# First mixer of a two-block model: gate and convolved projections as one stream of 28 three-pass tiles, with scan and norms inside it

## What is computed

```python
h = rms_norm(x, norm_in_gain) * (1.0 + scale) + shift
q, k, v, z_attn, xbc, dt_raw, z_ssm = jnp.split(h @ w_in, splits, axis=-1)
o = stick_breaking_attention(q, k, v)
y_attn = rms_norm(o, sb_norm_gain) * jax.nn.silu(z_attn)
xbc = jax.nn.silu(causal_depthwise_conv(xbc, conv_w, conv_b))     # 4 taps, 1536 channels
xs, b_ssm, c_ssm = jnp.split(xbc, ...)                            # 1024, 256, 256
dt = jax.nn.softplus(dt_raw + dt_bias); a = -jnp.exp(a_log)
y = ssd_scan(xs, dt, a, b_ssm, c_ssm, d_skip)                     # Mamba-2, chunked, 16 heads of 64
y_ssm = rms_norm(y * jax.nn.silu(z_ssm), ssm_norm_gain)
x = x + gate * (jnp.concatenate([y_attn, y_ssm], -1) @ w_out)
```

## Time and profile before

| | |
|---|---|
| median of 3 runs | 2508.65 us (2505.75 to 2510.89) |
| profiled execution | 2508.63 us, of which the span is 2506.8 us |
| mean granted TensorE clock | 0.928 of full speed |
| busy over the span | PE 2208.9 us, DVE 1297.9, ACT 751.9, POOL 164.7 |
| attention's end to first w_out matmul | 346.28 to 669.50 us of the span |

### The profile page before, as it was taken

The page is one execution under the profiler, slowest core; times in us unless marked ns, Lnnn a source line. Parts: engine busy times, 40 slices in busy tenths (PEclk is TensorE's granted clock), DMA queues, the critical chain, the costliest instruction groups (busy, mean ns, idle before and its releaser), DMA issues. The chain is left out here.

```text
span 2506.8 us, 36778 instructions
## 1 busy us (share of the span) xinstructions
PE 2208.9 (88%) x15962; PEld 1677.8 (67%) x15962; DVE 1297.9 (52%) x1857; ACT 751.9 (30%) x1098; POOL 164.7 (7%) x137
## 2 busy tenths in 40 slices
PE   6998998968796994999899799989894997999896
PEld 2885754766585861899826688878452665888784
DVE  2325733675335457545533667633377635676434
ACT  2334631222322442010012322222243633222222
POOL 0000000000000007211130000000003400000000
PEclk8998999978898996999979899999987998999998
DMA  6222001201131220000002132323320011323230
GB/s 251 101 93 76 1 19 66 77 9 34 52 100 61 101 70 0 4 4 4 16 17 68 59 100 94 101 79 98 101 70 1 1 59 42 99 95 100 78 100 34
DMA packets 45841, 158.79 MB, mean 63 GB/s; under 512 B 5120, under 2 KB 7168, under 8 KB 45552
## 3 DMA queue, kind: packets, MB, share of 16 engines
q1 hardware_dynamic: 43824, 150.84, 18.4%
q10 hardware_dynamic: 1856, 5.60, 0.6%
HBM read 154.28 MB, written 2.14 MB: 62 GB/s over the span
## 5 line engine op out<-in xcount | busy, mean ns | idle before, releaser
L883 PE MATMUL banks<-up_x_high,up_w_high 128*128 128x512 f32 x704 | 276.3, 392 | 29.1 <-DVE up_x_low L896 29.1
L884 PE MATMUL banks<-up_x_low,up_w_high 128*128 128x512 f32 x704 | 275.9, 392 | 0.0
L885 PE MATMUL banks<-up_x_high,up_w_low 128*128 128x512 f32 x704 | 275.6, 392 | 0.0
L866 DVE TENSOR_TENSOR up_w_low<-weight_ring,up_w_high 128x1024 fp32r<-128x1024 f32 x88 | 107.8, 1226 | 140.1 <-ACT up_w_high L861 140.1
L883 PEld LDWEIGHTS banks<-up_x_high,up_w_high 128*128 128x128 f32 x704 | 133.4, 190 | 58.5 <-issue 30.7
L904 DVE SCALAR_TENSOR_TENSOR act<-banks,cols,act 128x511 f32<-128x511 f32 (+2 forms) x212 | 158.8, 749 | 7.5
L885 PEld LDWEIGHTS banks<-up_x_high,up_w_low 128*128 128x128 f32 x704 | 133.4, 190 | 28.2
L884 PEld LDWEIGHTS banks<-up_x_low,up_w_high 128*128 128x128 f32 x704 | 133.5, 190 | 27.5
L318 PE MATMUL banks<-down_x_high,down_w_high 128*128 128x512 f32 x352 | 139.5, 396 | 13.1 <-DVE down_x_low L357 13.1
L861 ACT CAST up_w_high<-weight_ring 128x1024 fp32r<-128x1024 f32 x88 | 92.1, 1049 | 192.8 <-PE banks L885 188.4
L319 PE MATMUL banks<-down_x_low,down_w_high 128*128 128x512 f32 x352 | 139.1, 395 | 0.0
(11 more groups left out here) (445 smaller groups left out, 4814.0 us busy)
## 6 DMA issues: line engine op xcount, KB each, us to landing
weight_ring<-in_up SPq DMA_DIRECT2D x88, 512.0 KB, 3.6
weight_ring<-in_down SPq DMA_DIRECT2D x44, 512.0 KB, 3.6
weight_ring<-in_w_ada SPq DMA_DIRECT2D x24, 512.0 KB, 5.9
weight_ring<-in_w_rkv SPq DMA_DIRECT2D x24, 512.0 KB, 3.2
weight_ring<-in_w_in SPq DMA_DIRECT2D x20, 512.0 KB, 3.3
weight_ring<-in_w_out SPq DMA_DIRECT2D x16, 512.0 KB, 3.2
weight_ring<-in_w_q SPq DMA_DIRECT2D x8, 512.0 KB, 6.8
weight_ring<-in_w_k SPq DMA_DIRECT2D x8, 512.0 KB, 3.2
```

The source lines that it names most:

```text
L866: nc.vector.tensor_tensor(w_low[:, n % 2, :], ring[:, i % RING, :], w_high[:, n % 2, :].bitcast(f32), ALU.subtract).then_inc(wl_made, 1)
L883: nc.tensor.matmul(PS[:, n % 4, :], high, x_high[:, k, :], start=k == 0, stop=False)
L884: nc.tensor.matmul(PS[:, n % 4, :], high, x_low[:, k, :], start=False, stop=False)
L885: mm = nc.tensor.matmul(PS[:, n % 4, :], low, x_high[:, k, :], start=False, stop=k == 7)
```

## The change

Stages 1 to 7, up to w_out, become one block with one queue per engine, written out by hand. After dt, TensorE runs a stream of 28 three-pass tiles: 12 of xbc, 8 of z_ssm, 8 of z_attn (now three-pass too; z_ssm becomes tile-wise, with w_z laid out in tiles like the others). x_high and x_low of all eight tiles of h are made once and kept. The tiles z0 to z15 use banks 6 and 7. The scan's matmuls stand between gate tiles: per chunk the inputs with broadcasts 0 and 1, a gate tile, broadcasts 2 and 3, two gate tiles, the outputs and the state (pairs of heads interleaved). Broadcasts use two banks (4 and 5) in place of four. The sums of the attention norm follow tile 3, those of the scan's norm follow z13. VectorE makes w_low of tiles 0 and 1 alone; GpSimd makes the other 26 and multiplies y_attn by its gates. ScalarE makes a tile's w_high right after taking the tile two before it (take_z). norm_ssm is finished before the w_out block begins. Removed lines of the scan that return as they were are left out here, as is the rest that "..." stands for; take_z, high_of_weights and chunk are functions of ScalarE's queue.

```diff
         planned(A["w_ada"], range(16, 24), 8)
-        planned(A["w_in"], range(20), 8)
         planned(A["w_dt"], range(1), 8, 16)
+        planned(A["w_in"], range(8, 20), 8)
         planned(A["w_z"], range(8), 8)
+        planned(A["w_in"], range(8), 8)
         planned(A["w_out"], range(16), 8)
...
-        run_stage(norm_program("norm_sb", rows(o), 8, D, 1e-6, lambda i: col("sb_norm_gain", i), rows(y_attn), scratch=rows(F[4]))[0],
-                  gemm_program("z_attn", 8, 8, rows(h), {"act": lambda e, n, b: nc.scalar.activation(F[3][:, n, :], b, ACT.Silu)}))
-        multiply("gate_attn", y_attn[:, :, :], y_attn[:, :, :], F[3][:, :, :])
-        xs, bc = F[3], F[4]
-        run_stage(conv_program("xbc", 12, None, 4, lambda n, j: col("conv_w", j * 12 + n), lambda n: col("conv_b", n),
-                               lambda n: xs[:, n, :] if n < 8 else bc[:, n - 8, :], split=(*open_split("xbc", 5, KT), rows(h), None)))
...
+        y_attn, xs, bc = F[2], F[3], F[4]
+        x_high, x_low, w_high, w_low = open_split("hproj", 5, KT)
...
+        AFTER = [(1, 2, 3), (4, 5, 6), (7, 8, 9), (10, 11, 12)]
...
+        def gate(pool, j):
+            pool.wait_ge(z_taken, j + 1)
+            pool.wait_ge(o_scaled, j - 7)
+            nc.gpsimd.tensor_tensor(y_attn[:, j - 8, :], y_attn[:, j - 8, :], z_dst(j), ALU.mult).then_inc(z_gated, 1)
...
+                def passes(t, k, bank):
+                    high, low = (w[:, t % 2, k * P:(k + 1) * P] for w in (w_high, w_low))
+                    nc.tensor.matmul(PS[:, bank, :], high, x_high[:, k, :], start=k == 0, stop=False)
+                    nc.tensor.matmul(PS[:, bank, :], high, x_low[:, k, :], start=False, stop=False)
+                    return nc.tensor.matmul(PS[:, bank, :], low, x_high[:, k, :], start=False, stop=k == 7)
+
+                def z_tile(j):
+                    next_chunk(pe)
+                    pe.wait_ge(wl_made, N_XBC + j + 1)
+                    if j >= 2:
+                        pe.wait_ge(z_taken, j - 1)
+                    for k in range(8):
+                        mm = passes(N_XBC + j, k, 6 + j % 2)
+                    mm.then_inc(weight_used, 1)
...
+                def broadcasts(c, quarters):
+                    for q4 in quarters:
+                        if q4 >= 2:
+                            pe.wait_ge(sca[c], 4 + 2 * (q4 - 2))
+                            pe.wait_ge(vec[c], 7 + 2 * (q4 - 2))
...
+                    if c:
+                        pe.wait_ge(vec[c - 1], 29)
...
+                    if c:
+                        pe.wait_ge(vec[c - 1], 32)
+                    broadcasts(c, (0, 1))
...
+                def chunk_outputs(c):
+                    for pair in range(H // 2):
+                        if pair % 2 == 0:
+                            pe.wait_ge(vec[c], 15 + pair)
...
+                next_chunk(pe)
+                next_chunk(pe)
+                pe.wait_ge(wl_made, 2)
+                for k in range(8):
+                    pe.wait_ge(xl_made, k + 1)
+                    for t in range(2):
+                        mm = passes(t, k, t)
+                        if k == 7:
+                            mm.then_inc(weight_used, 1)
+                for t in range(2, N_XBC):
+                    next_chunk(pe)
+                    pe.wait_ge(wl_made, t + 1)
+                    if t >= 4:
+                        pe.wait_ge(conv_step, TAPS * (t - 3))
+                    for k in range(8):
+                        mm = passes(t, k, t % 4)
+                    mm.then_inc(weight_used, 1)
+                    if t == 3:
...
+                z_tile(0)
+                for c in range(NB):
+                    chunk_inputs(c)
+                    z_tile(AFTER[c][0])
+                    broadcasts(c, (2, 3))
+                    z_tile(AFTER[c][1])
+                    z_tile(AFTER[c][2])
+                    chunk_outputs(c)
+                z_tile(13)
...
+                z_tile(14)
+                z_tile(15)
...
+                def high_of_weights(t):
+                    i = first + 1 + t
+                    act.wait_ge(weight_loaded[i % RING], 16 * (i // RING + 1))
+                    if t >= 2:
+                        tile_done(act, t - 2)
+                    nc.scalar.copy(w_high[:, t % 2, :], ring[:, i % RING, :]).then_inc(wh_made, 1)
+
+                def take_z(j):
+                    tile_done(act, N_XBC + j)
+                    if j >= 11:
+                        act.wait_ge(z_gated, j - 10)
+                    nc.scalar.activation(z_dst(j), PS[:, 6 + j % 2, :], ACT.Silu).then_inc(z_taken, 1)
+                    if j + 2 < 16:
+                        high_of_weights(N_XBC + j + 2)
...
+                high_of_weights(0)
+                high_of_weights(1)
+                for k in range(8):
+                    nc.scalar.copy(x_high[:, k, :], h[:, k, :]).then_inc(xh_made, 1)
...
+                for i in range(8):
+                    nc.scalar.activation(sq_o(i), y_attn[:, i, :], ACT.Square, scale=D ** -0.5).then_inc(o_squared, 1)
+                for t in range(N_XBC):
+                    high_of_weights(t + 2)
...
+                    act.wait_ge(conv_step, TAPS * (t + 1))
+                    nc.scalar.activation(conv_dst(t), conv_dst(t), ACT.Silu).then_inc(conv_silu, 1)
+                take_z(0)
+                for c in range(NB):
+                    chunk(c)
+                    for j in AFTER[c]:
+                        take_z(j)
+                take_z(13)
+                for i in range(8):
+                    act.wait_ge(s_gated, i + 1)
+                    nc.scalar.activation(sq_o(i), y[:, i, :], ACT.Square, scale=D ** -0.5).then_inc(s_squared, 1)
+                act.wait_ge(s_summed, 1)
+                nc.scalar.activation(root, sum_bank, ACT.Abs_reciprocal_sqrt, bias=eps_col).then_inc(s_rooted, 1)
+                take_z(14)
+                take_z(15)
...
+                for n in range(N_XBC):
+                    convolve(n)
...
+                    if n >= 6 and n < 10:
+                        for i in (2 * (n - 6), 2 * (n - 6) + 1):
+                            nc.vector.scalar_tensor_tensor(out=y_attn[:, i, :], in0=y_attn[:, i, :], scalar=col("sb_norm_gain", i), in1=root,
+                                                           op0=ALU.mult, op1=ALU.mult).then_inc(o_scaled, 1)
...
+                for c in range(NB):
+                    chunk(c)
+                dve.wait_ge(z_taken, 8)
+                dve.wait_ge(vec[NB - 1], 29)
+                for i in range(8):
+                    nc.vector.tensor_tensor(y[:, i, :], y[:, i, :], z_ssm[i], ALU.mult).then_inc(s_gated, 1)
...
+            @block.gpsimd
+            def _(pool):
+                for t in range(2, N_TILES):
+                    pool.wait_ge(wh_made, t + 1)
+                    nc.gpsimd.tensor_tensor(w_low[:, t % 2, :], ring[:, (first + 1 + t) % RING, :], w_high[:, t % 2, :].bitcast(f32), ALU.subtract).then_inc(wl_made, 1)
+                    j = t - N_XBC - 2
+                    if j >= 8:
+                        gate(pool, j)
+                gate(pool, 14)
+                gate(pool, 15)
...
-        split_gemm("z_ssm", 8, rows(h), {"act": lambda e, n, b: nc.scalar.activation(F[3][:, n, :], b, ACT.Silu)})
-        multiply("gate_ssm", F[3][:, :, :], F[3][:, :, :], y[:, :, :])
...
-        run_stage(norm_ssm, split_chain("w_out",
+        run_stage(split_chain("w_out",
```

More of the change, by code:

```diff
@@ new lines, in program @@
+        sdt = flat(h)
+        state, x_dt, x_end = sdt[:, 0:1024], sdt[:, 1024:2048], sdt[:, 2048:3072]
+        b_tok, cb = sdt[:, 3072:3328], sdt[:, 3328:3584]
+        seg, c_exp = wide[:, 0:2048], wide[:, 2048:4096]
+        y = xs
+        z_ssm = [bc[:, 4 + i, :] for i in range(4)] + [aux[:, i * T:(i + 1) * T] for i in range(4)]
+        z_attn = [aux[:, (4 + i) * T:(5 + i) * T] for i in range(3)]
+        z_dst = lambda j: z_ssm[j] if j < 8 else z_attn[j % 3]
+        slot = lambda i: late[:, 512 + i * 64:576 + i * 64]
@@ new lines, in program @@
+        s_gated, s_squared, s_summed, s_rooted, s_fixed, s_scaled = (sem("norm_ssm_" + n) for n in ("gated", "squared", "summed", "rooted", "fixed", "scaled"))
+        cums, moved, cbs, broad, vec, sca, outs, states = (
+            [sem(f"scan{c}_{n}") for c in range(NB)] for n in ("cums", "moved", "cb", "broadcast", "vec", "act", "y_ready", "state_ready"))
+        first = at["used"]
+        tile_done = lambda eng, t: eng.wait_ge(weight_used, first + 2 + t)
+        TAPS = 4
+        conv_dst = lambda n: xs[:, n, :] if n < 8 else bc[:, n - 8, :]
@@ L1105, in program @@
[L1105 to L1112 removed]
+        restore("after_ssd")
```

278 lines of the change are left out of this document (155 added, 123 removed).

## The result

The changed kernel takes 2440.34 us (median of four runs, 2437.52 to 2441.42) against 2509.77 for the kernel before, timed beside it: a ratio of 0.9724, 95% interval 0.9707 to 0.9741. The forecast was 2439.6. Its profiled execution was timed at 2441.42 us.

What follows compares the result with a forecast made beforehand. One stage, from attention's end to w_out's first matmul, took 323.2 us with TensorE busy only 260; eleven terms along TensorE's queue summed to 254.2, 69.0 less, so 2508.6 became 2439.6 us, range 2422 to 2462.

Steps and rivals of the forecast that it cites:

- Step 1: Start of the stage: 0.2 us, then 64 step-size matmuls with the clock falling halfway, 10.4; sum 10.6 us.
- Steps 2 and 3: TensorE's stream of 28 tiles x 24 matmuls x 0.227, 152.3 us; first matmuls at half clock, 2.7 us.
- Step 4: Before tile 2: no cover for its cast and Pool's subtraction (time P, 2.4 us), a stall of 3.1 us.
- Step 5: Sums of squares of the attention norm, with the squares done before: 7.0 us.
- Step 6: Scan matmuls on TensorE: 11.0 us a chunk, four chunks less the last state update, 42.3 us.
- Step 7: Each chunk's third gate tile waits for ScalarE's late cast and Pool's low part: 2.7 us, x4 = 10.8.
- Step 9: TensorE clock drops after six stalls of 2 to 4 us, 1.6 each: 9.6 us.
- B: Rival: gaps of 2 to 3 us need not drop the clock, dt at full clock; 2424 us, chance 0.15.
- Steps 10 and 11: Stage's end: wait for squares 2.3 and sums 6.9; last SiLU, gate, join and w_out weight split 5.5 us.
- Rival C: Pool's subtraction slower than its line, by fp32r output or lock; with P = 5, 2460 us; chance 0.12.
- D: Rival: the scan does not slip under the stream, outputs pushed past the third tile; 2467 us, chance 0.07.
- E: Rival: Pool's subtraction rules, deciding from P = 10 us; 2516 us, slower from there on; chance 0.03.

Runs made afterwards that it cites:

- the early cast: Changed kernel with ScalarE casting each chunk's third gate tile's weights between the second and third quarters' exponentials; 2426.7 us, ratio 0.9672.
- The second execution: Changed kernel run once more, unaltered, to see which waits drop the TensorE clock; 2440.8 us, ratio 0.9717 to the kernel before.
- the scan apart: Changed kernel with all gate tiles up to tile 12 run before the scan, none between the parts of a chunk; 2462.3 us, ratio 0.9807.

## Why the prediction was right

The total was right within 1 us, and that closeness is partly luck. The mechanisms held (one stream, the stall before tile 2, the wait for the third gate tile, the scan under the tiles), but errors of 5 us met in opposite directions, and the time of the same code outside the stage varies by up to 10 us from one execution to the next. Step by step, from the windows above, forecast first:

- Step 1, start and step sizes: 10.6, measured 11.4. The clock fell earlier than half way; 10.97 us for the 64 matmuls lie in the bounds 6.9 to 13.8.
- Steps 2 and 3: tiles 0 and 1 13.6, measured 13.9; the nine tiles of the convolved row 49.0, measured 49.4. There the pitch of 0.227 stands, as does the count. In the scan it does not quite: the twelve gate tiles, at 24 x 0.227 = 5.44 each 65.3, took 67.7 without their waits and the clock drop. In the third chunk they took 5.59, 5.72 and 5.65. A tile that begins behind other matmuls or a wait costs 0.1 to 0.3 more than one that follows a tile, and step 2 had no term for it: 2.4 too little.
- Step 4, the stall before tile 2: 3.1, measured 3.03, released by GpSimd as said. P was 2.34 to 2.4 alone, so an fp32r output on GpSimd costs no more than f32 by the line through the earlier trace rows.
- Step 5: 7.0, measured 6.5.
- Step 6, the scan's matmuls: 42.3, measured 41.9 (10.8, 11.0, 11.0 and, without the last state update, 9.1; the rows of the third chunk are below). The 11.0 a chunk, with the 3.4 us taken off for the half clock, was right.
- Step 7, the third gate tile: 4 x 2.7, measured 4 x 3.0. The profile names no releaser there, not GpSimd's low part as I had written, but the early cast showed that the cause is the named one.
- Step 8, the wait for the state update: 1.1, measured 0.3, once.
- Step 9, clock drops: six at 1.6, 9.6. This is the term that failed. The profiled execution had two in these places: the one in the fourth chunk cost 1.6, as sized, and the one at tile 2 cost 3.0 (tiles 2 and 3 took 13.88 instead of 10.9). Together 4.6, so the term was 5.0 too large. The second execution had four, in all four chunks, and its stage was 3.0 longer. The error was to make a rule out of it, a drop after every stall; what the runs show is a chance, 19 of 42 for waits of 1.9 to 3.0 us, that differs from execution to execution, and a cost of 1.6 to 3.0. B's other half, that these stalls never drop it, is wrong too.
- Steps 10 and 11: the wait for the squares 2.3, measured 2.15; sums 6.9, measured 6.6; z14 and z15 10.9, measured 11.5; the wait before w_out 5.5, measured 5.34.

The third chunk's own matmuls (windows of TensorE alone, columns as in the earlier trace rows; the gate tiles lie between and are left out):

```profile
506.04:509.84 3.80, 3.80 (x35) 1.00 0.01 4
515.43:517.13 1.70, 1.70 (x18) 1.00 0.31 51
531.50:536.97 5.47, 5.47 (x69) 1.00 0.28 99
```

So 5.0 too much for the clock and 0.6 in all the rest met 2.4 too little for the gate tiles in the scan, 1.2 for the third tiles' waits and 0.8 at the start, and the stage came out 1.2 us under the forecast.

The lock between GpSimd and VectorE was charged at 0.4 a chunk, the rest taken as slack, and I had it the wrong way round: the multiplications were to be held to about S+20 by the subtraction. They were not held; they ended at S+17.3 (461.73 in the first chunk), and the subtraction, which began 1.2 us before that, took 3.4 instead of 2.4. That one is on TensorE's path, so the charge should have been 1; the three tenths by which the wait passed 2.7 are part of that. Its reverse, VectorE held by GpSimd, showed where the slack is thin: the clamp at 2.23 instead of 0.43 in the kernel with the early cast. The Trainium skill's lock ("SBUF — State Buffer", section "SBUF: two separate sides") covers the subtraction and the multiplications, which have two SBUF inputs: 3.41 against 2.4. The price of 2.4 a chunk worked out from it was not paid, since only the last 1.2 us of the multiplications lay over the subtraction. The clamp has one SBUF input, and no row says in which mode it ran.

Rival C was under-priced (2460 forecast for P = 5, 2470 measured at 4.8), because a longer GpSimd step also stands before the state update and drops the clock. D was refuted by the scan apart. E needs P over 10 and was not tried.

What the move of the low parts to GpSimd brings was not priced apart in the prediction, and the runs answer it: nothing that the order of VectorE's queue could not bring. Of what the whole change brings, 69 us, the scan under the stream has 20 by the scan apart. The rest is only read from rows, not taken apart by a run: z_attn took 55.07 us for products that cost 8 x 5.44 = 43.5 in three passes; the pitch of the convolved part no longer contains taps, SiLU, cast and low part in a row, 5.44 for about 6; and most joins are gone.

## What to carry to other kernels

When one engine's stream is the path, list what each of its pieces waits for, and move the helper instruction that stands behind another engine's long run to the front of it: here one cast moved ahead in ScalarE's queue took away 10 us of waits, and 13.7 of 2440 us as timed. Before giving a step to another engine, look whether it lies on a ring through the present one's queue; the order may be all that is wrong. And price a clock drop after a wait of 2 to 3 us as a chance (here a little under one half), not a rule.

## What the hardware showed that was not expected

- Under matmuls of 16 columns the granted clock went from 1.00 to 0.50 with TensorE busy without a gap (12.00 of 12.00 us, then 6.00 of 6.00).
- One wait of 3.00 us, in the same place of the same program, was followed by a clock of 1.00 in one execution and 0.50 in another; at the low clock tile 2 lost 3.0 us, the tile in the fourth chunk 1.6.
- A clamp on VectorE with one SBUF input and one constant, 0.43 us alone, was held to 2.23 by a GpSimd subtraction.
